# An encoder layer between attention and feed-forward: group scaling on ScalarE, first gate/up weights loaded early, and the normalised tile's transposes between the halves of each product

## The reference, cut to what matters

```python
mix = jnp.concatenate([_rms_norm(o_a, grp_norm_a), _rms_norm(o_m, grp_norm_b)], axis=-1) @ w_out
x = _layer_norm(alpha * x + g1 * mix, ln1_g, ln1_b)
u2 = _layer_norm(x) * (1 + sc2) + sh2
f = (jax.nn.silu(u2 @ w_gate) * (u2 @ w_up)) @ w_down
return _layer_norm(alpha * x + g2 * f, ln2_g, ln2_b)
```

## Time and profile before

| | us |
|---|---|
| median of three runs (lowest, highest) | 1913.42 (1912.98, 1916.4) |
| the profiled execution | 1913.25 |
| its span | 1911.4 |
| TensorE busy in the span | 1753.3 (92%) |
| VectorE busy | 1157.3 (61%) |
| ScalarE busy | 697.4 (36%) |

### The profile page before, as it was taken

One profiled execution on the slowest core, in us unless ns is written; L12 is line 12 of the kernel. 1 busy time (PEld: TensorE's weight loads), 2 busy tenths in 40 slices (PEclk: granted clock), 3 DMA queues, 4 the chain that ended last, 5 costly groups with the idle time before them and its releaser, 6 DMA issues. The chain is left out here.

```text
span 1911.4 us, 22485 instructions
## 1 busy us (share of the span) xinstructions
PE 1753.3 (92%) x8562; PEld 1385.3 (72%) x8562; DVE 1157.3 (61%) x1401; ACT 697.4 (36%) x1081; POOL 217.8 (11%) x230
## 2 busy tenths in 40 slices
PE   4998963999999999898799999999999999999993
PEld 2898842666667777677688888887888878878872
DVE  3788774878778876698643444334434344344388
ACT  3566551767667667553411111111111111111114
POOL 1123432100212220000000000000000000000063
PEclk7999976999999999999899999999999999999997
DMA  9133457545635451432311111111111111111123
GB/s 361 43 118 112 125 166 163 165 139 171 167 82 140 109 118 38 154 116 78 121 53 36 33 33 33 44 33 33 36 51 33 33 33 44 33 33 33 56 88 132
DMA packets 132087, 171.54 MB, mean 90 GB/s; under 512 B 17721, under 2 KB 104793, under 8 KB 128945
## 3 DMA queue, kind: packets, MB, share of 16 engines
q1 hardware_dynamic: 114896, 104.96, 17.9%
q0 software_dynamic: 12288, 46.25, 9.5%
q10 hardware_dynamic: 4832, 19.42, 3.2%
HBM read 128.21 MB, written 42.30 MB: 89 GB/s over the span
## 5 line engine op out<-in xcount | busy, mean ns | idle before, releaser
L1995 DVE TENSOR_TENSOR sum_f<-pair,sum_f 128x1024 f32<-128x1024 f32 x200 | 244.0, 1220 | 474.6 <-PE pair L172 473.1
L170 PE MATMUL pair<-u_hi,w_out_hi 128*128 128x512 f32 (+1 forms) x1056 | 377.3, 357 | 12.2 <-DVE w_out_hi L1623 12.2
L172 PE MATMUL pair<-u_hi,w_out_hi 128*128 128x512 f32 (+1 forms) x1056 | 376.8, 357 | 0.0
L171 PE MATMUL pair<-u_lo,w_out_hi 128*128 128x512 f32 (+1 forms) x1056 | 376.6, 357 | 0.0
L1843 ACT ACTIVATE silu_gate<-pair 128x512 f32<-128x512 f32 (+1 forms) x63 | 33.2, 527 | 581.6 <-PE pair L172 581.6
L170 PEld LDWEIGHTS pair<-u_hi,w_out_hi 128*128 128x128 f32 x1056 | 198.8, 188 | 45.1 <-DVE w_out_hi L1623 12.4
L171 PEld LDWEIGHTS pair<-u_lo,w_out_hi 128*128 128x128 f32 x1056 | 198.9, 188 | 32.9
L172 PEld LDWEIGHTS pair<-u_hi,w_out_hi 128*128 128x128 f32 x1056 | 198.8, 188 | 32.4
L1193 ACT ACTIVATE p_f<-pair 128x1024 f32<-128x1024 f32 (+1 forms) x144 | 140.8, 978 | 155.0 <-PE pair L1073 83.9
L1244 DVE TENSOR_TENSOR p_lo<-p_f,p_hi 128x1024 fp32r<-128x1024 f32 (+1 forms) x144 | 167.2, 1162 | 42.4 <-ACT p_hi L1197 42.0
L170 PE MATMUL pair<-down_hi,hidden_hi 128*128 128x512 f32 x440 | 182.2, 414 | 9.7 <-DVEq L1966 6.1
(11 more groups left out here) (249 smaller groups left out, 2869.9 us busy)
## 6 DMA issues: line engine op xcount, KB each, us to landing
w_ada_late<-in_w_ada ACTq DMA_DIRECT2D x16, 1024.0 KB, 4.9
gate_up_raw<-in_w_gate SPq DMA_DIRECT2D x21, 512.0 KB, 4.0
gate_up_raw<-in_w_up SPq DMA_DIRECT2D x21, 512.0 KB, 5.2
down_raw<-in_w_down SPq DMA_DIRECT2D x21, 512.0 KB, 3.2
w_ada_first<-in_w_ada SPq DMA_DIRECT2D x8, 1024.0 KB, 14.2
o_tile<-o SPq DMA_DIRECT2D x10, 512.0 KB, 4.1
x<-y SPq DMA_DIRECT2D x10, 512.0 KB, 2.6
gate_up_raw<-x SPq DMA_DIRECT2D x10, 512.0 KB, 3.6
```

What stands on the lines that cost most here:

```text
L170: pe.matmul(out, a[0], b[0], start=start, stop=False)
L171: pe.matmul(out, a[0], b[1], start=False, stop=False)
L172: return pe.matmul(out, a[1], b[0], start=False, stop=stop)
L1995: dve.tensor_tensor(sumf[:, t, :], src, sumf[:, t, :], ALU.add).then_inc(dn_added, 1)
```

## The change

Four things move, all in `output` and the first slice of `channel`.

1. ScalarE scales the attention tile (`group_scale`), VectorE only inverts (`group_inverse`).
2. ScalarE's `mix_hi` of a turn stands ahead of `modulate`.
3. On TensorE `u_t` of a tile stands between the two halves of a later mix product; the last two stand between the halves of chunks 0 and 1 of slice 0.
4. The first gate and up weights go to a tile of their own, in the memory of the attention tiles, loaded by SP as soon as the last of these is transposed. Their high parts are written after the first half of the last mix product, the low parts follow VectorE's last addition for tile 8. For this the slices of gate and up lie in `w_out`'s columns, slot 0 in the first 512 columns of each row block.

```diff
-                flat = k.wo[0][:, :, :].rearrange("p a b -> p (a b)")
-                k.wgu = [flat[:, m * 4 * D:(m + 1) * 4 * D].rearrange("p (s m j c) -> p s m j c", s=2, m=2, c=P) for m in range(2)]
+                columns = k.wo[0][:, :, :].rearrange("p j (s h m c) -> p h s m j c", s=2, h=2, m=2)
+                k.wgu = [columns[:, h, :, :, :, :] for h in range(2)]
...
+    first_gu = at(36 * KB, "gate_up_first", [P, 2, KT, P])
...
+            if n == NT - 1:
+                sp.wait_ge(mt_tr, 2 * NT)
+                for m, name in enumerate(("w_gate", "w_up")):
+                    sp.dma_start(first_gu[:, m, :, :], rows(k.i[name][0])[:, :, 0:P]).then_inc(k.gu_in, 16)
...
+        def mix(t):
+            pe.wait_ge(mt_lo, 2 * (t + 1))
+            pe.wait_ge(mix_free, t - 1)
+            ins = mix_half(t, 0)
+            if t == NT - 1:
+                ins.then_inc(half_done, 1)
+            if t >= 2:
+                u_t(t - 2)
+            mix_half(t, 1).then_inc(mix_ready, 1)
...
-        k.last_u_t = lambda: u_t(NT - 1)
+        k.late_u_t = [lambda: u_t(NT - 2), lambda: u_t(NT - 1)]
...
         for n in TURNS[3:]:
-            if 0 <= n - 3 < NT - 1:
-                u_t(n - 3)
             if n < NT:
                 mix_t(n)
             if 0 <= n - 1 < NT:
...
+        def group_scale(t):
+            act.wait_ge(ss_inverted, t + 1)
+            for m in range(2):
+                ins = act.activation(ot[:, t % 3, m * 512:(m + 1) * 512], ot[:, t % 3, m * 512:(m + 1) * 512], ACT.Copy, scale=ss[:, t % 3, m:m + 1])
+            ins.then_inc(on_ready, 1)
...
-                for m, name in enumerate(("w_gate", "w_up")):
-                    act.dma_start(k.raw_gu[:, m, :, :], rows(k.i[name][0])[:, :, 0:P]).then_inc(k.gu_in, 16)
                 act.dma_start(k.raw_d[:, :], k.i["w_down"][0][0:P, :]).then_inc(k.down_in, 16)
+            if n < NT:
+                mix_hi(n)
             if 0 <= n - 3 < NT:
                 modulate(n - 3)
-            if n < NT:
-                mix_hi(n)
             if 0 <= n - 2 < NT:
                 root(n - 2, 0)
             for t in {0: [1], 1: [2, 3]}.get(n, [n + 2] if n + 2 < NT else []):
                 k.squares(act, t)
                 group_root(t)
-            if n == NT + 1:
+                if t < 3:
+                    group_scale(t)
+            if 3 <= n + 1 < NT:
+                group_scale(n + 1)
+            if n == NT:
+                act.wait_ge(half_done, 1)
                 act.wait_ge(k.gu_in, 32)
-                act.activation(k.wgu[0][:, 0, :, :, :], k.raw_gu[:, :, :, :], ACT.Copy).then_inc(k.gu_hi, 1)
+                for m in range(2):
+                    ins = act.activation(k.wgu[0][:, 0, m, :, :], first_gu[:, m, :, :], ACT.Copy)
+                ins.then_inc(k.gu_hi, 1)
...
-        def group_norm(t):
+        def group_inverse(t):
             dve.wait_ge(ss_ready, t + 1)
-            link(dve.reciprocal(ss[:, t % 3, :], ss[:, t % 3, :]))
-            for m in range(2):
-                ins = dve.tensor_scalar(ot[:, t % 3, m * 512:(m + 1) * 512], ot[:, t % 3, m * 512:(m + 1) * 512],
-                                        ss[:, t % 3, m:m + 1], None, ALU.mult)
-            ins.then_inc(on_ready, 1)
+            dve.reciprocal(ss[:, t % 3, :], ss[:, t % 3, :]).then_inc(ss_inverted, 1)
...
+            if t == NT - 2:
+                dve.wait_ge(k.gu_hi, 1)
+                for m in range(2):
+                    ins = dve.tensor_tensor(k.wgu[1][:, 0, m, :, :], first_gu[:, m, :, :], k.wgu[0][:, 0, m, :, :], ALU.subtract)
+                ins.then_inc(k.gu_lo, 1)
...
+                    if first and m == 0 and c < 2:
+                        k.late_u_t[c]()
                 mm.then_inc(gu_ready, 1)
-                if first and c == 0:
-                    k.last_u_t()
```

More of the change, by code:

```diff
@@ L1359, in output @@
     mt, ss, ot, o_in = [mt_hi, mt_lo], k.grp_sums, k.ot, k.o_in
+    first_gu = at(36 * KB, "gate_up_first", [P, 2, KT, P])
+    half_done = k.sem("mix_half_done")
     tabs_in, g1_in, modp = k.sem("oc_tabs_in"), k.sem("oc_gate_in"), k.sem("oc_mod_plus_one")
     x_in = [k.sem(f"oc_x_in{s}") for s in range(2)]
-    ss_ready, on_ready = k.sem("ss_ready"), k.sem("on_ready")
+    ss_ready, ss_inverted, on_ready = k.sem("ss_ready"), k.sem("ss_inverted"), k.sem("on_ready")
     mt_tr, mt_hi, mt_lo = k.sem("mt_tr"), k.sem("mt_hi"), k.sem("mt_lo")
@@ L1437, in mix_half, with u_t @@
             return mm
+        def u_t(t):
+            pe.wait_ge(xh_ready, t + 1)
+            if t == 0:
+                pe.wait_ge(k.o_free, 48)
+            if t >= 1:
+                pe.wait_ge(uf_ready, t)
+            for j in range(KT):
+                mm = pe.transpose(k.bank[3][:, j // 4, j % 4 * P:(j % 4 + 1) * P], r[:, j * P:(j + 1) * P], k.ident[:, :])
+            mm.then_inc(u_tr, 1)
         def mix(t):
@@ L1441, in mix @@
             pe.wait_ge(mix_free, t - 1)
-            mix_half(t, 0)
+            ins = mix_half(t, 0)
[3 more added lines that the diff above has]
+                u_t(t - 2)
             mix_half(t, 1).then_inc(mix_ready, 1)
@@ L1518, in _ @@
         group_root(0)
+        group_scale(0)
         k.take_last()
@@ L1597, in u_low @@
             dve.tensor_tensor(k.u2[1][:, :, cols], uf[:, :, :], k.u2[0][:, :, cols], ALU.subtract).then_inc(u2_ready, 1)
-        group_norm(0)
+        group_inverse(0)
         mix_lo(0)
         k.normalise_last()
-        group_norm(1)
+        group_inverse(1)
         mix_lo(1)
-        group_norm(2)
+        group_inverse(2)
         dve.wait_ge(tabs_in, 96)
@@ L1610, in _ @@
             if 3 <= n < NT - 1:
-                group_norm(n + 1)
+                group_inverse(n + 1)
             if 0 <= n - 2 < NT:
@@ L1614, in _ @@
             if n == 2:
-                group_norm(3)
+                group_inverse(3)
             if n < NT:
@@ L1619, in _ @@
                 first_norm(n - 2)
-            if n == NT + 1:
-                dve.wait_ge(k.gu_hi, 1)
-                dve.tensor_tensor(k.wgu[1][:, 0, :, :, :], k.raw_gu[:, :, :, :], k.wgu[0][:, 0, :, :, :], ALU.subtract).then_inc(k.gu_lo, 1)
             if 0 <= n - 3 < NT:
@@ L1708, in load @@
             sp.dma_start(raw_d[:, :], k.i["w_down"][0][bass.ds(f * P, P), :]).then_inc(d_in, 16)
+        sp.wait_ge(k.mix_ready, NT)
         load(1)
```

## The result

The changed kernel takes 1920.24 us (median of 7 runs, 1916.55 to 1921.49) against 1914.5 us before (7 runs): ratio 1.0026, 95% interval 1.0015 to 1.0036. It is slower by about a quarter of a per cent. The profiled execution took 1916.55 us, the lowest of the seven, for a span of 1914.7 us; that is 3.3 us over the profiled one of before.

The account below looks back on a forecast made before the run. The stage was taken as bound by a loop of VectorE, TensorE's transposes, then VectorE, with ScalarE having spare time. 6.8 + 5.6 - 7.8 = +4.6 us on 1913.25 gave 1917.9 us, range 1909.2 to 1922.5.

Parts of the forecast that it names:

- The scaling on ScalarE: Group scaling of an attention tile, moved to ScalarE: 0.7 us for each operation, 1.3 us a pair, range 1.07 to 2.2.
- low end of 1.07 us: Shortest time allowed for ScalarE's scaling pair, from two 128x512 copies out of PSUM without a factor from memory.
- not-slower rival: Clock holds at all gaps, the end's too: 1910.2 us, 1909.0 with a quick scaling pair; chance 0.12 with other gains.
- TensorE's wait: Before the mix transposes, TensorE stands 2.1 us for ScalarE's scaling; turns become 15.0 us, five turns +4.3 us.
- The clock: In the five stalling turns, 3.5 of five gaps drop TensorE to 1.2 GHz, 1.6 us each: +5.6 us, range 0 to 8.0.
- The start: First normalised tile's transposes come behind mix transposes and half a product, and the first scaling costs more: +3.0 us.
- The end: Early gate and up weights let chunk 2 start sooner after tile 8's gating multiply begins: gain 7.8 us.
- VectorE's order sets this, not the transfer: First chunk's start follows VectorE's weight subtraction behind tile 8's last add; a load 2 us late would cost about 1 us.
- The sum: Whole change: 6.8 us later at tile 8's gating multiply, plus 5.6 for the clock, less 7.8 gained: +4.6 us.
- all five gaps fall: Clock falls in all five stalling turns: +7.0 us, 1920.3 us; chance 0.20 together with a slower scaling.
- clock held in the turns: TensorE's 2.1 us gaps in the turns cost no clock: -1.0 us, 1912.3 us; chance 0.20.
- The change doesn't do what it says: Weights land late, first chunk starts as late as VectorE's end of tile 9, most of 7.8 us lost: some 1924; chance 0.03.

Follow-up runs that it names:

- scale_first: Changed kernel with ScalarE's scaling of the next attention tile moved directly behind the mix tile's copy, ahead of the modulation: 1907.15 us.
- transposes_ahead: Changed kernel with normalised tiles 0 to 7 transposed ahead of the mix transposes again, as before the change; ScalarE's late scaling stays: 1905.9 us.
- filled_gap: Changed kernel with 18 unread identity transposes on TensorE ahead of the mix transposes in the five stalling turns: 1913.04 us.
- late_weights: Changed kernel with the first weights' copies and low part, and the transposes of tiles 8 and 9, where they stood before; load still early: 1926.23 us.

## Why the prediction came out as it did

1917.9 us was forecast, inside a range of 1909.2 to 1922.5; the median is 1920.24. The mechanism was the forecast one, and the working can be compared term by term with the profiled execution, against whose kind of time it was made.

- **The scaling on ScalarE.** Taken as 0.7 us each and 1.3 us a pair from a row of the same size; L1502 takes 0.71 us each and 1.32 us a pair. The Trainium skill's estimate (ScalarE: Activation LUTs, What ACT_TABLE_LOAD costs), 706 ns, agrees with the 0.71 us. The low end of 1.07 us, and with it the part of the not-slower rival that hung on it, was not seen.
- **TensorE's wait.** Forecast 2.1 us, measured 2.14, 2.14, 2.13, 2.12 and 2.11 us in the five turns, each released by L1502. The turn without a fall: forecast 15.0, measured 15.1. The two later turns: forecast 13.87, measured 13.74. Shown by scale_first and transposes_ahead, which take the wait away from either side.
- **The clock.** 3.5 of five gaps were to cost 1.6 us each, 5.6 us in all. In the profiled execution three fell, at 1.6 us each: 4.8 us. filled_gap shows that the 1.6 us are the clock's and the rest of the turn's loss is not. The Trainium skill (TensorE: Matmul & The Clock Gate, HAM oscillation) describes a loop that loses the clock in every turn behind waits of some 3 to 5 us. Two of the five turns here, behind waits of 2.1 us like the others', held 1.00; that all five must fall by this page was more than it states, since its waits are longer. late_weights, with the same five waits, had four of five turns of 16.6 us or more.
- **The start.** Forecast 3.0 us, measured 2.6 (A to tile 1's gating multiply). The 2.67 us gap is gone, as the working had it: TensorE runs through to tile 0's transposes, which come half a product later.
- **The end, the term that was mis-sized.** Forecast 7.8 us, measured 6.9 (U to S), 6.0 between the medians with and without it. The first chunk was to start at U+10.45 and starts at U+11.1. The step that failed is "VectorE's order sets this, not the transfer": the working had the load's issue right to half a microsecond, but no duration for the transfer. VectorE's last add of tile 8 ends at 926.50, and L1610 starts at 927.08, 0.57 us behind it and as soon as ScalarE's copies are done, which had waited for the weights to land. A second size was off as well: the first half of the first chunk was to take 4.2 us and takes 4.84 (929.49 to 934.33), because TensorE runs it at 1.2 GHz for 4.2 us; before, the stretch at 1.2 GHz behind the 12.16 us gap was 2.9 us long. Both together put tile 9's gating multiply at U+17.1, not U+15.8, and its transposes at U+29.0, not U+27.6; from there to chunk 2 it is 8.3 us where 8.9 were forecast. Chunk 2 starts at 955.70, U+37.3, not U+36.5.
- **The sum.** 2.63 + 9.44 - 0.80 - 6.90 = +4.37 us from A to S, forecast +4.6. That it fits this well is in part luck: the terms were off by -0.4 (start), -0.5 (five turns with their falls), -0.3 (two turns) and +0.9 us (end), which nearly cancel. The profiled execution shows +3.3 because it came to A 1.1 us earlier than before's, in a part of the program that the change leaves alone; over the nine profiled kernels A lies between 774.8 and 777.2 us. From S on nothing was lost, as the working had it, though the second weights' load now waits on SP for the last mix product (`sp.wait_ge(k.mix_ready, NT)`, a line of the change that is not among those shown ahead of the prediction).
- **The median.** The forecast was made for an execution with three or four falls. The medians differ by 5.7 us, not 3.3. The two quickest of the seven runs (1916.55 and 1916.96 us) have a granted clock of 0.967, the other five (1919.31 to 1921.49) one of 0.962 to 0.964: the two falls that the profiled one was spared, at 1.6 us each, would be 3.2 of the 3.7 us between it and the median. Only the first of them has a trace, so that this is the cause is argued and not shown. Two falls, 3.4 us each at half rate, would lower the mean clock by an estimated 0.002, less than the 0.003 to 0.005 seen, so other stretches differ too. From the other side, filled_gap, which has no falls in the turns, lies 7.2 us under the changed kernel's median, as much as four to five falls cost. By that the usual execution has four to five falls, between the 3.5 forecast and the rival "all five gaps fall", 1920.3 us; the forecast is 2.3 us under the median.

Of the rivals, "clock held in the turns" would have read 1912.3 us; filled_gap, in which the clock is held by other means, took 1913.04. "The change doesn't do what it says" is ruled out by the first chunk at U+11.1 and by late_weights.

## What to carry to other kernels

Work moved to an engine with spare time is priced by its place in that engine's queue, not by the spare time: ask when its result is ready and when the reader now comes for it. Two edits that are each free can spend the same cover; here one put the scaling late on ScalarE and the other brought its reader forward by 8.4 us, and only together did they pass each other. When two edits share a hand-over, time each of them alone as well as together. The same question of place holds for a queue of transfers: the early weights were issued some 20 us after their memory was free, because of what stood ahead of them on SP.

## What the runs showed of the hardware that was not expected

Waits of 2.1 us on TensorE, equal to 0.03 us, in the same place of equal turns, cost the clock in three turns of one execution and not in the two before them; how many fell differs between executions (three here, four in late_weights). A slow stretch of the third turn, with the stretches around it, TensorE busy in the whole of it:

```profile
842.00:848.40 6.40, 4.27 (x20) 3.21 (x18) 6.19 (x10) 5.94 (x14) 0.00 (x0) 1.00 0.07 28
848.40:851.85 3.45, 3.45 (x12) 3.07 (x13) 3.31 (x6) 0.45 (x2) 0.00 (x0) 0.51 0.38 152
851.85:860.00 8.15, 8.15 (x41) 6.82 (x40) 3.95 (x6) 3.31 (x10) 0.00 (x0) 1.00 0.37 129
```

The granted clock fell as TensorE took up work after the wait, to 1.2 GHz, and was back at 2.4 GHz 3.4 us later. Transposes that nobody reads, put into the wait, kept it at 1.00 in all five turns of filled_gap.
